# Where the down product of the previous expert pass stands inside an expert pass

## The reference

```python
    def expert_block(args):
        xb, e = args
        hcat = xb @ w13[e]
        hid = jax.nn.silu(hcat[:, :EXPERT_FF]) * hcat[:, EXPERT_FF:]
        return hid @ w2[e]
```

## Time and profile before

| | |
|---|---|
| median of 3 runs | 3589.38 us (3588.7 to 3593.16) |
| the profiled execution | 3585.89 us, its span 3584.1 us |
| PE busy over the span | 3156.5 us (88%) |
| expert stage of layer 0, from the first product to the end of the last | 638.7 to 1121.7 us |
| expert stage of layer 1 | 1558.2 to 2040.5 us |
| HBM traffic over the span | 620.49 MB by DMA packets |

### The profile page before, as it was taken

The page is one execution under the profiler, slowest core; times in us unless marked ns, Lnnn a source line. Parts: engine busy times, 40 slices in busy tenths (PEclk is TensorE's granted clock), DMA queues, the critical chain, the costliest instruction groups (busy, mean ns, idle before and its releaser), DMA issues. The chain is left out here.

```text
span 3584.1 us, 39885 instructions
## 1 busy us (share of the span) xinstructions
PE 3156.5 (88%) x16263; PEld 1609.2 (45%) x16263; DVE 991.0 (28%) x2006; ACT 769.6 (21%) x1592; POOL 317.9 (9%) x306
## 2 busy tenths in 40 slices
PE   8998997978685998788776679999999979999999
PEld 4446963322222446333222245565544435556444
DVE  2425634100003007330000121265400220176202
ACT  1412250100001006110000143245400012245200
POOL 0015410200001000120000101100000001100000
PEclk9999998989887999899898889999999999999999
DMA  6431524899997432379999731201011111111121
GB/s 207 170 130 59 207 82 185 351 427 414 416 412 295 144 143 41 106 299 427 418 408 422 314 100 39 56 22 48 24 47 47 59 47 41 47 45 48 48 85 44
DMA packets 170762, 620.49 MB, mean 173 GB/s; under 512 B 70062, under 2 KB 72524, under 8 KB 144592
## 3 DMA queue, kind: packets, MB, share of 16 engines
q1 hardware_dynamic: 143952, 463.07, 34.3%
q10 hardware_dynamic: 8064, 114.30, 7.6%
q0 software_dynamic: 18560, 40.50, 3.2%
HBM read 584.41 MB, written 60.76 MB: 180 GB/s over the span
## 5 line engine op out<-in xcount | busy, mean ns | idle before, releaser
L1568 PE MATMUL banks<-weight_ring,experts_xT 128*32 128x512 f32 (+1 forms) x2240 | 359.2, 603 | 27.6 <-DMA weight_ring<-in_moe_w 16.5
L1586 PE MATMUL banks<-weight_ring,experts_hT 128*32 128x512 f32 (+1 forms) x1216 | 261.5, 661 | 114.5 <-DMA weight_ring<-in_moe_w 112.6
L2616 PE MATMUL banks<-weight_ring,cols 128*128 128x512 f32 x672 | 294.6, 600 | 14.2 <-PEq L2755 8.2
L1586 PE MATMUL banks<-cols,experts_hT 128*32 128x512 f32 (+1 forms) x448 | 177.7, 672 | 46.9 <-DMA cols<-in_moe_w 46.9
L2616 PE MATMUL banks<-weight_ring 128*128 128x512 f32 x480 | 207.0, 593 | 3.7 <-PEq L2594 1.9
L2616 PEld LDWEIGHTS banks<-weight_ring,cols 128*128 128x128 f32 x672 | 128.8, 192 | 178.5 <-issue 178.5
L1568 PEld LDWEIGHTS banks<-weight_ring,experts_xT 128*32 128x32 f32 (+1 forms) x2240 | 107.5, 118 | 225.7 <-issue 217.8
L3124 PE MATMUL banks<-cols,weight_ring 128*128 128x512 f32 x416 | 182.9, 592 | 1.9 <-PEq L285 1.9
L1586 PEld LDWEIGHTS banks<-weight_ring,experts_hT 128*32 128x32 f32 (+1 forms) x1216 | 73.3, 128 | 240.3 <-DMA weight_ring<-in_moe_w 126.6
L665 PE MATMUL banks<-cols,weight_ring 128*128 128x512 f32 x384 | 170.1, 598 | 1.1 <-PEq L285 1.1
L2852 ACT ACTIVATE pairs_p<-banks,pairs_low 128x768 f32<-128x768 f32 (+1 forms) x160 | 130.5, 815 | 180.9 <-DVE pairs_low L2907 88.0
(11 more groups left out here) (456 smaller groups left out, 4489.2 us busy)
## 6 DMA issues: line engine op xcount, KB each, us to landing
weight_ring<-in_moe_w SPq DMA_DIRECT2D x96, 2048.0 KB, 22.4
weight_ring<-in_moe_w ACTq DMA_DIRECT2D x36, 2048.0 KB, 16.7
cols<-in_moe_w SPq DMA_DIRECT2D x22, 2048.0 KB, 23.5
experts_slot<-in_moe_w SPq DMA_DIRECT2D x20, 2048.0 KB, 24.2
cols<-in_moe_w ACTq DMA_DIRECT2D x18, 2048.0 KB, 16.3
weight_ring<-in_w_in SPq DMA_DIRECT2D x16, 2048.0 KB, 8.0
weight_ring<-in_w_ada SPq DMA_DIRECT2D x12, 2048.0 KB, 11.4
weight_ring<-in_a_w_in SPq DMA_DIRECT2D x8, 2048.0 KB, 11.8
```

What stands on the lines that cost most here:

```text
L1568: mm = pe.matmul(bank[a:a + n, :], self.xT[:, 4 * part + k, a:a + n], slots(r, part)[:, k, c:c + 512], start=part == k == 0, stop=part == ...
L1586: mm = pe.matmul(self.out[c][a:a + n, :], self.hT[:, f, a:a + n], slots(r, 2)[:, f, c * 512:c * 512 + 512], start=f == 0, stop=f == 3)
L2616: mm = pe.matmul(ps[i % 8][0:u.shape[0], 0:u.shape[1]], u.lhs(w, k), u.rhs(w, k), start=k == 0, stop=k == u.kd - 1)
```

## The change

From pass 2 on, the down product of p-1 moves ahead of the second half of gate and up of p: in the products on PE, in the order in which weights are loaded (and so in which slot each takes and which engine issues it), and in the evictions on ACT and DVE. Passes 0 and 1 and the end of the stage keep their code.

```diff
+def down_before_up(p):
+    return p >= SELECTED
+
 def weight_uses():
     out = []
     for p in range(NP + 1):
-        if p < NP:
-            out += [(r, part, ("first_half", "up")[part], p) for part in range(2) for _, _, r in reversed(PASSES[p].tiles)]
-        if p:
-            out += [(r, 2, "down", p - 1) for _, _, r in reversed(PASSES[p - 1].tiles)]
+        first, up = ([(r, part, ("first_half", "up")[part], p) for _, _, r in reversed(PASSES[p].tiles)] if p < NP else [] for part in range(2))
+        down = [(r, 2, "down", p - 1) for _, _, r in reversed(PASSES[p - 1].tiles)] if p else []
+        out += first + (down + up if down_before_up(p) else up + down)
     return out
...
+                    if p and down_before_up(p):
+                        weights_landed(PASSES[p - 1].tiles, 2, "down", p - 1)
+                        B.down(pe, p - 1, PASSES[p - 1].tiles, slots)
                     weights_landed(tiles, 1, "up", p)
                     B.gate_up(pe, tiles, 1, slots)
...
-                    if p:
+                    if p and not down_before_up(p):
                         weights_landed(PASSES[p - 1].tiles, 2, "down", p - 1)
                         B.down(pe, p - 1, PASSES[p - 1].tiles, slots)
...
-                    B.gated(act, p)
-                    if p + 1 < NP:
-                        B.take_cols(act, p + 1)
-                    if p:
+                    def results():
                         B.other_half_y(act, p - 1)
                         for m, q in behind_down.items():
                             if q == p - 1:
                                 load_weights(act, m, expert)
+                    if p and down_before_up(p):
+                        results()
+                    B.gated(act, p)
+                    if p + 1 < NP:
+                        B.take_cols(act, p + 1)
+                    if p and not down_before_up(p):
+                        results()
...
+                    if p and down_before_up(p):
+                        B.half_y(dve, p - 1)
                     B.hidden(dve, p)
-                    if p:
+                    if p and not down_before_up(p):
                         B.half_y(dve, p - 1)
```

## The result

The changed kernel is slower: its median is 3607.32 us against 3593.16 us of the kernel before, measured side by side; the ratio is 1.0042, with a 95% interval of 1.0031 to 1.0053. The prediction was 3588 us, no difference to be told, with a range up to 3603. It was built on the earlier median of 3589.38 us; 3.8 of the 19 us between forecast and measurement are that the kernel before, too, took longer when it was measured beside the change. The profiled execution of the changed kernel took 3611.22 us, its span 3609.4.

The account below looks back on a forecast made before the run. Weight loads were taken to bound the expert stages, with PE following. The sum -2 + 0 + 0 on 3585.9 us gave 3583.9; the median lies 3.5 us higher, so 3587.4, given as 3588 us, range 3577 to 3603.

Parts of the forecast that it names:

- What bounds the kernel: Both expert stages: weight loads are the bound, DMA engines busy 0.99 of the time, and PE follows them.
- PE's clock did not become the bound: Rival in the expert stages: added cold starts keep PE's clock from recovering and PE bounds, 3613 us; chance 0.13.
- (a) The seam: Between passes, PE newly waits 1.7 us for the input copy, 26 times, 44 us in all, hidden by weight waits.
- (b) The spread of the waits: PE's weight waits become more and shorter, slots return more evenly; gain 2 us of 8.8 us dry DMA time.
- the term of -2 us in the sum: The gain taken for more even return of slots in the expert stages, out of 8.8 us of dry DMA time.
- the first-half tiles of 9, 11, 13 and 15: Rival: these tiles come late, PE waits 8 us, DMA dries 1 to 2 us at eight places, 3601 us; chance 0.10.
- The sign that was named for being right: DMA share of 0.98 to 1.00 in the middle of both expert stages, of 442 us or so.
- (c) Cold starts: In two four-tile passes, five more cold product phases cost 12.5 us of PE, fitting in 13.1 spare; taken as nothing.
- (d) The end: End of each expert stage, down 14 now ahead of the second half of 15: 0 a layer, between -5 and +2.5 us.
- the bare chain of 3.2 us: Behind the second half of 15: silu, multiplication, transposes, copy and hops uncovered, 3.2 us, of which 1.6 showed before.

Follow-up runs that it names:

- the even passes alone: Down product of p-1 ahead of the second half of p only in passes 6, 8, 10, 12 and 14, against the kernel before: 0.9984, 3582.47 us.
- the odd ones alone: Down product of p-1 ahead of the second half of p only in passes 7, 9, 11 and 13, against the kernel before: 1.0309, 3699.49 us.
- three kernels with eight loads of one step: Against the kernel before: only the order of loads changed, 1.0305; only products and evictions changed, 1.0416; only passes 7, 9, 11 and 13 changed, 1.0309.
- the exchange of tiles: Changed kernel with loads 52, 64, 76 and 88 each exchanged with the load two behind; against the kernel before 1.003.
- the end as before: Changed kernel with pass 15 put back, its second half ahead of down 14; against the kernel before 1.0024, 3600.07 us.
- The control: The kernel before run once more, unchanged, for a second profile: 1.0002, stages 484.7 and 484.0 us.
- the run of pass 2's evictions: Changed kernel with pass 2's evictions of down 1 back behind silu and the input copy; against the kernel before 1.0065, 3612.18 us.

## Why the prediction was wrong

**What bounds the kernel** held: PE is busy 193 and 191 of the 260 us in which the time is lost, as before (192 and 192), while the DMA engines move less. PE's clock did not become the bound: it was granted 0.90 and 0.86 against 0.87 and 0.88. The loss is in dry DMA time, and in the end.

**(a) The seam** was right in place, size and cover: nine new waits of 1.75 us in layer 0, the other four seams covered by the waits for weights ahead of 9, 11, 13 and 15, and without them the stages are only 3.2 and 3.3 us shorter. It was not quite free, but at 6.5 of the 29 us by which the stages grew it isn't what made the change slow.

**(b) The spread of the waits** is the step that failed. The waits did spread, and I took it that slots are then given back more evenly, for a gain of 2 us. The four-tile passes lost 8.5 and 12.8 us of transfer time instead, and the term of -2 us in the sum should have been a loss. The sentence was about the mean wait; what the traces point to is the tightest load, since SP issues in order and one slot that is late holds every load behind it. I had that mechanism as a rival (the first-half tiles of 9, 11, 13 and 15, a wait of 8 us each; measured 9) and gave it 0.10, because "five or six other loads are in flight then". The trace after shows the flaw: the loads in flight at the start of the wait are used up by its end, since SP issues nothing for 41 us. With the even passes alone SP stands at the same load for 35.8 us (932.92 to 968.67), and over the last 11 us of that the share is still 1.01: it is the last few us that cost. The rival's price of 1 to 2 us a place was low too: over 967 to 978 the share lacks 0.27 of 11 us, 3 us at this one place, and 1.8 us at the next. Its sentence that before "a phase more lay between" misses that before those tiles had five steps, and that other loads, the second-half tiles of 9, 11, 13 and 15, had the two.

The kernel before has as many loads of distance two. Its tight one on ACT (load 66) landed 9.2 us after its issue, where the changed kernel's load 64 took 14.7, and the product that used it waited 1.60 us there. One other load was in flight when load 66 was issued (it landed at 957.05); with load 64, beside one that landed at 952.84, there were two that landed at 960.38 and 971.24. That the loss is gone with the even passes alone, and that the odd ones alone cost 3.1%, fits the distance from the freeing of a slot to the use of its next load, and rules out a price for each moved product. The count does not give the time: three kernels with eight loads of one step cost 3.05, 4.16 and 3.09%. Why the same count of twos costs 0.24% more in the one arrangement than in the other I have only read from one place of the trace, and no run changes that place alone; the exchange of tiles that was to do it did not bring them sooner. That part of the cause stays open.

The sign that was named for being right was too coarse to tell: over 665 to 1109 us the changed kernel has a share of 0.99, within the 0.98 to 1.00 asked for, though 0.01 of 444 us is 4.4 us.

**(c) Cold starts** were mis-sized only slightly. In two passes the changed kernel has two (9.99 and 8.58 us instead of 7.07, behind waits of 8.98 and 4.43 us), before one; PE is busy 49.60 us instead of 47.13, and the spare time covers it. None follows the new waits at the seam: behind 1.75 us a phase takes 7.07 to 7.09 us. Short idles can do it all the same: at the end of the stage the last down product, with idles of 1.49 and 0.94 us on either side of four transposes ahead of it, took 8.62 us at a granted clock of 0.82, and 8.77 in layer 1. The Trainium skill (TensorE: Matmul & The Clock Gate) has two rules on this. Its section on HAM oscillation says that matmul groups between waits for DMA start cold each time; the trace agrees for these waits of 4.43 and 8.98 us. Its section on a second failure mode says that frequent short idles between groups cost the clock too; the trace doesn't show that for a single idle of 1.75 us, and is in line with it for the two idles at the end of the stage; in the kernel before, with the 0.94 us alone, that product took 7.07 us.

**(d) The end** was mis-sized: forecast -5 to +2.5 us a layer, measured +5.0 and +3.2 behind the last landing, 0.18% of the whole. The forecast's own terms, 7.6 (by its sum 7.4) to 14.8 us plus up to 3 against 15.6, reach from -8 to +2.2. It let the second half of 15 start as soon as its tiles were in. They were in at 1109.5; but the late first half ended only at 1108.5 and down 14 stands next, so that it started at 1116.98. Behind it lies the bare chain of 3.2 us, as forecast, with waits of 1.49 and 0.94 us, and then a down product that is cold (8.62 us), 1.6 us for which the forecast had no term. With the end as before the second half comes first and down 14 covers that chain.

**What stays open.** The stages of the profiled executions grew by 29 us together, the median by 14. The control's profile has stages of 968.7 us in a span of 3597.0, that of the kernel before 965.2 in 3584.1: the stages repeat within 4 us, what lies outside them varies by 9 us from one execution to another, and nothing that I ran says why. That the run of pass 2's evictions has shorter stages and a longer median stays open with it. Among the medians, differences under some 0.15% are read with that in mind.

## What to carry to other kernels

When loads go through a ring of slots in a fixed order, don't ask how long the waits are on the mean after a reordering: list for each load the phase that frees its slot and the phase that first uses it, and look at the shortest distances; here three steps instead of two for eight loads took away a loss of 0.24%, and one instead of two cost 3.1%. The list would not have been enough here: both kernels have twelve loads of two steps, and one was 0.42% slower. Ask of each tight load, too, what is in flight when it is issued and which loads stand behind it. The order of the loads and the order of use belong together: either alone cost 3 to 4%. At the end of a streamed stage, put last what needs the last bytes, and keep a product that has its data to stand over the chain of small steps.

## What the runs showed that I had not expected

An in-order issue queue hides a late slot for as long as the transfers ahead of it last, and then shows all of it at once: SP stood for 41 us, and only the last few of them cost. With the even passes alone it stood at the same load for 35.8 us, and the share of the DMA engines stayed at 1.01. The time from issue to landing says how full the queues are: 7.5 us for 2 MB where they had run dry, 14.7 us on ACT beside two of its own, 33.9 us for a load at the end of SP's row; so issuing a load earlier on a full queue did not bring it earlier. The Trainium skill (DMA: Bandwidth & Descriptors, on issuing engines that are not separate DMA queues) says that issuing from several engines saves only issuing time; here the choice of the engine also bore on the landing. In the changed kernel's trace a load that ACT issued at 952.37 landed at 967.11, ahead of one that SP had issued at 936.88 and that landed at 971.24. And a scatter of result rows on which nothing waits in most passes held up one eviction in each layer of one run, on ACT for 23.5 us in layer 0.
